# Two-layer hybrid trunk with a hierarchical mixture of experts: routing over all 32 experts at once, and a first quad fed in smaller steps

## The chip, the cores and the metric

The kernel runs on one core of one Trainium2 chip. The metric is the device time of one execution in microseconds. Several executions agree within about 0.2 per cent.

## The reference, cut to what matters

```python
D_MODEL, SEQ, DEPTH = 1024, 256, 2
N_EXPERT_GROUPS, EXPERTS_PER_GROUP, TOP_K, D_EXPERT = 4, 8, 2, 256

def hier_moe(h, w_rg, w_re, w_gate, w_up, w_down):
    t = h.reshape(b * s, d)
    pg = jax.nn.softmax((t @ w_rg).astype(jnp.float32), -1)
    pg_top, g_idx = lax.top_k(pg, 1)
    le = (t @ w_re).astype(jnp.float32).reshape(-1, N_EXPERT_GROUPS, EXPERTS_PER_GROUP)
    le_sel = jnp.take_along_axis(le, g_idx[:, :, None], axis=1)[:, 0]
    pe_top, e_idx = lax.top_k(jax.nn.softmax(le_sel, -1), TOP_K)
    w = pg_top * pe_top / jnp.sum(pe_top, -1, keepdims=True)
    ids = g_idx * EXPERTS_PER_GROUP + e_idx
    combine = jnp.sum(jax.nn.one_hot(ids, N_EXPERTS, dtype=jnp.float32) * w[..., None], 1)
    hg = jnp.einsum("nd,edf->nef", t, w_gate)
    hu = jnp.einsum("nd,edf->nef", t, w_up)
    a = jax.nn.silu(hg) * hu * combine[..., None].astype(t.dtype)
    return jnp.einsum("nef,efd->nd", a, w_down).reshape(b, s, d)

def reference(x, ...):
    for l in range(DEPTH):
        ...                                  # three gated mixer branches and w_out
        x = x + hier_moe(rms_norm(x, norm2_g[l]), w_router_group[l], w_router_expert[l],
                         w_expert_gate[l], w_expert_up[l], w_expert_down[l])
    return rms_norm(x, norm_f_g)
```

Everything is float32. One expert has three matrices of 1 MB each (1 MB is 1,048,576 bytes here), so the 32 experts of a layer are 96 MB.

## The kernel before

The program is written engine by engine with semaphores by hand; what stands in one engine's block runs in that order. Each layer is a `trunk_stage` (projection, the three mixer branches, output projection) and an `expert_stage`.

**Slots.** Expert matrices stream from DRAM into a ring of 20 places of 1 MB (`RING_E`). SyncE (SP) issues every load with `load_expert` in the order of a counter `pos`, 96 positions for a layer. A quad is four experts, and it has 12 positions: eight for gate and up matrices, four for down matrices. Positions 0 to 19 are loaded while the trunk still runs, wherever a part of the arena comes free. Position 20 goes into the place of position 0, and so on: `quads_sp` waits until TensorE has used a place, then issues the next load. For the first quad it waits for `gu_part` (positions 20 to 25) and `gu_ready` (26, 27), then for the down products `y_ready` (28 to 31); positions 32 to 39 wait for `gu_ready` of the second quad.

**The first eight positions** are cut differently (`SPLIT_LOADS`): each place holds half of the contraction blocks of two experts, gate and up, so that places 0 and 1 serve the first two of the eight contraction blocks k. Each place is filled by two loads of 512 KB, with runs of 2 KB.

**Routing** is a chain on VectorE (DVE) in `route_dve`, where `link` makes each instruction wait for the one before: group argmax, `gmask`, masked logits `big`, a sum over groups into `les`, top 2 by MAX8 and FIND_INDEX8, `pick`, `either`, `sel`. TensorE (PE) turns `sel` into ranks, and DVE builds the `onehot` matrices of the first two quads (L2079). Before `sel` is there, PE runs warm-up matmuls (`keep_clock`, L340). ScalarE (ACT) meanwhile loads two tables and computes the router's exponentials (L1670).

**The first quad** (`first_quad`): PE gathers the tokens of the four experts, one k at a time, into PSUM (`gather_pair`, L1863); ACT (L1803) or DVE (L2089) copies a pair of k to `xsel`, times the gain, and PE multiplies by the gate and up matrices (`gate_up_pair`, L1876). Pairs 0 and 2 are emptied by ACT and pairs 1 and 3 by DVE. Then follow `spread(0)` (L1913), which needs `comb_ready` from DVE's `combine_weights` (L1752 to L1766), `gather(1)` and `down(0)`.

The order of the first quad on PE before (rows of PE's program, layer 0; L1863 gathers, L1876 multiplies by gate and up, a product is one row per expert and k):

```order
L1863 MATMUL ps<-onehot,work 128x128 [waits x_copied,onehot_ready0]
L1863 MATMUL ps<-onehot,work 128x128 x7
L1876 MATMUL ps<-ring_rest,rows 32x512 [waits first_act0,expert_in0]
L1876 MATMUL ps<-ring_rest,rows 32x512 x7
L1863 MATMUL ps<-onehot,work 128x128 x4
L1876 MATMUL ps<-arena,rows 32x512 [waits first_dve0]
L1876 MATMUL ps<-arena,rows 32x512 x7
L1863 MATMUL ps<-onehot,work 128x128 x4
L1876 MATMUL ps<-arena,rows 32x512 [waits first_act0,expert_in1]
L1876 MATMUL ps<-arena,rows 32x512 x7
L1876 MATMUL ps<-arena,rows 32x512 [waits first_dve0]
L1913 MATMUL ps<-ident,onehot 128x128 [waits comb_ready]
```

All four gathers of k 0 to 3 stand ahead of the first product, and nothing stands between the products of pair 2 and those of pair 3.

Of the kernel before, what the change touches and what calls it, by code (L numbers as in the profile page):

```python
# [77 lines left out]
def trunk_program(nc, x, positions, norm1_g, w_in, b_in, attn_sinks, sgu_ln_g, sgu_ln_b, w_spatial,  # L78
# [7 lines left out]
    with ExitStack() as whole:  # L86
# [33 lines left out]
        idx_iota = sb("idx_iota", [P, PER_GROUP])  # L120
# [13 lines left out]
        with ExitStack() as ctx:  # L134
            ring_rest = sb("ring_rest", [P, (RING_E - RING_A) * SLOT], F32, ctx)
            rest_slots = ring_rest[:].rearrange("p (s n) -> p s n", n=SLOT)
            rows = sb("rows", [P, 2 * D], F32, ctx)
            h2t = rows[:].rearrange("p (k s) -> p k s", k=KB)
            xsel = rows[:, 0:D].rearrange("p (k s) -> p k s", k=KB)
            y = rows[:, D:2 * D]  # L140
            onehot = sb("onehot", [P, 2, TB, QUAD], F32, ctx)
            st_r = sb("st", [P, 2, S], F32R, ctx)
            st = st_r[:].bitcast(F32)
            acts = sb("acts", [P, 4 * F], F32, ctx)
            sg, a_sb = acts[:, 0:F], acts[:, F:2 * F]
# [6 lines left out]
            gmask = sb("gmask", [P, TB, GROUPS], F32, ctx)  # L152
            les = sb("les", [P, TB, 8], F32, ctx)
# [4 lines left out]
            pick = sb("pick", [P, TB, 2, 8], F32, ctx)  # L158
            either = sb("either", [P, TB, 8], F32, ctx)
            weighted = sb("weighted", [P, TB, 2, 8], F32, ctx)  # L160
# [18 lines left out]
        with ExitStack() as ctx:  # L179
# [10 lines left out]
            iota8_i = sb("iota8_i", [P, PER_GROUP], I32, ctx)  # L190
# [173 lines left out]
        def setup_pool(pool, link):  # L364

            pool.iota(dist_i[:, 0:P], pattern=[[-1, P]], base=0, channel_multiplier=1)
            pool.iota(dist_i[:, P:3 * P], pattern=[[-1, 2 * P]], base=P, channel_multiplier=1).then_inc(consts_ready, 1)
            link(pool.memset(ident[:], 0.0))
            pool.affine_select(out=ident[:], in_=ident[:], compare_op=ALU.not_equal, fill=1.0,
                               base=0, pattern=[[-1, P]], channel_multiplier=1).then_inc(consts_ready, 1)  # L370
            pool.iota(iota_i[:], pattern=[[1, EC]], base=1, channel_multiplier=0)
            pool.iota(iota8_i[:], pattern=[[1, PER_GROUP]], base=0, channel_multiplier=0)
# [34 lines left out]
        def rope_angles(dve, link):  # L407
# [26 lines left out]
            dve.tensor_copy(idx_iota[:], iota8_i[:])  # L434
# [16 lines left out]

        LAST_DOWN = LAYER_LOADS - 1
# [1189 lines left out]
        def expert_stage(l):  # L1642
# [62 lines left out]
            def over_groups(t):  # L1705
                return bcast(t.unsqueeze(2), [P, TB, GROUPS, PER_GROUP])

            def route_dve(dve, link):
# [16 lines left out]
                dve.max(etop[:, 0, :], les[:, 0, :])  # L1725
                link(dve.max(etop[:, 1, :], les[:, 1, :]))
                dve.max_index(top_i[:, 0, :], etop[:, 0, :], les[:, 0, :])
                link(dve.max_index(top_i[:, 1, :], etop[:, 1, :], les[:, 1, :]))
                link(dve.tensor_tensor(pick[:], bcast(idx_iota[:].unsqueeze(1).unsqueeze(1), [P, TB, 2, 8]),
                                       bcast(top_i[:, :, 0:2].unsqueeze(3), [P, TB, 2, 8]), ALU.is_equal))  # L1730
# [18 lines left out]
            def combine_weights(dve, link):  # L1749
# [8 lines left out]
                link(dve.tensor_tensor(weighted[:], pick[:], bcast(w12[:].unsqueeze(3), [P, TB, 2, 8]), ALU.mult))  # L1758
                link(dve.tensor_tensor(either[:], weighted[:, :, 0, :], weighted[:, :, 1, :], ALU.add))
                for tb in range(TB):  # L1760
                    dve.tensor_tensor(comb[:, tb, :, 0:4].rearrange("p (g h) e -> p g h e", h=2),
                                      bcast(either[:, tb, :].rearrange("p (h e) -> p h e", h=2).unsqueeze(1),
                                            [P, GROUPS, 2, 4]),
                                      bcast(gmask[:, tb, :].unsqueeze(2).unsqueeze(3), [P, GROUPS, 2, 4]),
                                      ALU.mult)
# [31 lines left out]
            def quads_act(act, R, a, b, routed):  # L1797
                def gathered(n):
                    if n == 0:
                        for i in (0, 2):  # L1800
                            act.wait_ge(R.first_ready, i + 1)
                            for k in (2 * i, 2 * i + 1):
                                last = act.activation(xsel[:, k, :], ps[:, 2 + i, (k % 2) * QUAD:(k % 2 + 1) * QUAD],  # L1803
                                                      ACT.Copy, scale=gain2[:, k:k + 1])
                            last.then_inc(R.first_act, 1)
# [9 lines left out]
                for n in range(a, b):  # L1815
# [16 lines left out]
                    if n == LAST:  # L1832
                        act.wait_ge(R.gu_part, 4)
# [24 lines left out]
            def quads_pe(pe, R, a, b, routed):  # L1858
                def gather_pair(i):

                    for k in (2 * i, 2 * i + 1):
                        for tb in range(TB):
                            mm = pe.matmul(ps[:, 2 + i, (k % 2) * QUAD:(k % 2 + 1) * QUAD],  # L1863
                                           work[:, tb, k * P:(k + 1) * P], onehot[:, 0, tb, :],
                                           start=(tb == 0), stop=(tb == 1))
                    mm.then_inc(R.first_ready, 1)

                def gate_up_pair(i):
# [3 lines left out]
                    pe.wait_ge(R.first_dve if i % 2 else R.first_act, i // 2 + 1)  # L1872
                    for k in (2 * i, 2 * i + 1):
                        for e in range(4):
                            w = first_parts(places(2 * i + e // 2)[:, 0, :])[:, e % 2, :, (k % 2) * F:(k % 2 + 1) * F]
                            mm = pe.matmul(ps[e * EC:(e + 1) * EC, 0, :].rearrange("p (a f) -> p a f", a=2),  # L1876
                                           xsel[:, k, e * EC:(e + 1) * EC], w, start=(k == 0), stop=(k == KB - 1),
                                           skip_group_check=True)
                    mm.then_inc(R.gu_part if i < 3 else R.gu_ready, 1)

                def first_quad():
# [3 lines left out]
                    gather_pair(0)  # L1885
                    gather_pair(1)
                    gate_up_pair(0)
                    gather_pair(2)
                    gate_up_pair(1)
                    gather_pair(3)  # L1890
                    gate_up_pair(2)
                    gate_up_pair(3)

                def gather(n):
                    pe.wait_ge(R.onehot_ready, n + 1)
                    if n == 1:
                        pe.wait_ge(R.first_act, 2)
                        pe.wait_ge(R.first_dve, 2)
# [173 lines left out]
            def quads_dve(dve, link, R, a, b, routed):  # L2072
# [11 lines left out]
                def gathered(n):  # L2084
                    if n == 0:
                        for i in (1, 3):
                            dve.wait_ge(R.first_ready, i + 1)
                            for k in (2 * i, 2 * i + 1):
                                last = dve.tensor_scalar(xsel[:, k, :], ps[:, 2 + i, (k % 2) * QUAD:(k % 2 + 1) * QUAD],  # L2089
                                                         gain2[:, k:k + 1], None, ALU.mult)  # L2090
                            last.then_inc(R.first_dve, 1)
# [242 lines left out]
```

## Time and profile before

| what | value |
|---|---|
| median of three runs | 1046.15 us (1045.91 to 1047.91) |
| the profiled execution | 1048.12 us, its span 1046.4 us |
| TensorE busy | 958.8 us (92%) |
| VectorE busy | 576.2 us (55%) |
| ScalarE busy | 426.7 us (41%) |
| moved by DMA | 313.04 MB, 299 GB/s on average |
| mean granted TensorE clock | 0.972 |

Times in the trace are microseconds from the span's start. Layer 0's expert stage lies at about 320 to 523 us, layer 1's at about 837 to 1040 us. "DMA share" is the busy share of the 16 DMA engines; it can read slightly over 1. The busy share of an engine is a mean over stages with different limits: the trunk keeps TensorE busy nearly all the time, the expert stages keep the DMA engines so.

### The profile page before, as it was taken

Reading aid. Unit: us, or ns where it says so; the run is one execution under the profiler, and the core shown is the slowest. Engines: PE = TensorE matmul, PEld = TensorE weight load, DVE = VectorE, ACT = ScalarE, POOL = GpSimd, SP = SyncE. Lnnn points to the kernel's source line nnn. Section 1 sums busy time; section 2 is a strip of 40 time slices with the busy share of each in tenths; the row PEclk is TensorE's granted clock in tenths of the full one; section 3 lists DMA queues with packets and bytes.
Section 4 is the critical chain, followed back from the end, with each engine's and each line's share of the span. In section 5 each row is a group of like instructions: output and inputs, shape, how many; then the busy total and the mean of one; then the engine's idle time right before and its main releaser. Section 6 shows DMA issues by size and latency. Waiting matters only on the chain.

```text
span 1046.4 us, 15393 instructions
## 1 busy us (share of the span) xinstructions
PE 958.8 (92%) x5894; PEld 668.5 (64%) x5894; DVE 576.2 (55%) x1186; ACT 426.7 (41%) x907; POOL 58.1 (6%) x74
## 2 busy tenths in 40 slices
PE   8999999999999986887899999999999999867786
PEld 6888877778886431533488887777788954333333
DVE  6765788886873321111176668898869542122212
ACT  5434566666443210111363355666664431111122
POOL 1030400000010000000003004000000100000000
PEclk9999999999999999888999999999999999989889
DMA  9965633247999999999998556332588999999996
GB/s 345 350 218 188 198 122 123 80 127 269 321 396 385 425 424 425 419 425 425 413 342 292 190 177 195 122 121 81 163 289 315 396 405 424 425 422 423 426 423 256
DMA packets 97114, 313.04 MB, mean 299 GB/s; under 512 B 13424, under 2 KB 18576, under 8 KB 74512
## 3 DMA queue, kind: packets, MB, share of 16 engines
q1 hardware_dynamic: 96704, 312.04, 78.7%
q8 instruction: 45, 0.74, 0.3%
q14 instruction: 29, 0.24, 0.1%
q10 hardware_dynamic: 336, 0.02, 0.0%
HBM read 310.20 MB, written 1.84 MB: 298 GB/s over the span
## 4 chain that ended last, share of the span: by engine, by line
PE 63%; DMA 16%; SPq 9%; DVE 6%; ACT 4%; issue 1%; DVEq 0%; ACTq 0%
PE ps L1354 14%; PE ps L1356 14%; PE ps L1355 14%; DMA arena<-in_w_expert_up_dram 10%; SPq L470 9%; DMA ring_rest<-in_w_expert_up_dram 5%; PE ps L1928 5%; PE ps L1452 2%; PE ps L1460 2%; PE ps L1903 1%; PE ps L1992 1%; PE ps L1876 1%; ACT probs L928 1%; DVE wlo L1038 1%; PE ps L1475 1%
## 5 line engine op out<-in xcount | busy, mean ns | idle before, releaser
L1354 PE MATMUL ps<-whi,ahi 128*128 128x512 f32 (+1 forms) x768 | 297.3, 387 | 6.5 <-DVE wlo L1038 5.1
L1356 PE MATMUL ps<-whi,alo 128*128 128x512 f32 (+1 forms) x768 | 289.6, 377 | 0.0
L1355 PE MATMUL ps<-wlo,ahi 128*128 128x512 f32 (+1 forms) x768 | 289.2, 377 | 0.0
L1038 DVE TENSOR_TENSOR wlo<-arena,whi 128x512 fp32r<-128x512 f32 (+1 forms) x352 | 231.5, 697 | 92.0 <-ACT whi L848 89.5
L848 ACT CAST whi<-arena 128x1024 fp32r<-128x1024 f32 (+1 forms) x176 | 180.6, 1029 | 186.5 <-PE ps L1356 186.5
L1354 PEld LDWEIGHTS ps<-whi,ahi 128*128 128x128 f32 x768 | 144.5, 188 | 38.0 <-DVE wlo L1038 7.9
L1356 PEld LDWEIGHTS ps<-whi,alo 128*128 128x128 f32 x768 | 144.4, 188 | 27.0
L1355 PEld LDWEIGHTS ps<-wlo,ahi 128*128 128x128 f32 x768 | 144.7, 188 | 24.4
L1928 PE MATMUL ps<-ring_rest,rows 128*32 128x512 f32 x320 | 95.2, 642 | 26.1 <-DMA arena<-in_w_expert_up_dram 26.1
L1928 PE MATMUL ps<-arena,rows 128*32 128x512 f32 x448 | 95.2, 662 | 10.5 <-DMA arena<-in_w_expert_up_dram 8.9
L2120 DVE SCALAR_TENSOR_TENSOR acts<-ps,wslot,acts 128x256 f32<-128x256 f32 x16 | 7.7, 484 | 162.3 <-ACT acts L1838 137.5
L1903 PE MATMUL ps<-onehot,work 128*128 128x128 f32 x448 | 58.5, 293 | 17.5 <-issue 9.1
L1838 ACT ACTIVATE acts<-ps,rslot 128x256 f32<-128x256 f32 x16 | 7.6, 475 | 161.4 <-PE ps L1928 158.5
L1903 PEld LDWEIGHTS ps<-onehot,work 128*128 128x128 f32 x448 | 55.8, 206 | 27.6 <-issue 18.3
L928 ACT ACTIVATE probs<-probs,neg 128x128 f32<-128x128 f32 x112 | 49.5, 444 | 32.7 <-DVE neg L1163 32.7
L1928 PEld LDWEIGHTS ps<-ring_rest,rows 128*32 128x32 f32 x320 | 23.2, 117 | 61.5 <-issue 61.5
L2004 PE MATMUL ps<-rows,st 128*128 128x512 f32 x112 | 54.9, 612 | 0.2
L2104 DVE TENSOR_TENSOR xs<-ps,xs 128x512 f32<-128x512 f32 x56 | 38.7, 692 | 22.7 <-PE ps L2004 22.7
L1928 PEld LDWEIGHTS ps<-arena,rows 128*32 128x32 f32 x448 | 24.3, 121 | 39.9 <-issue 39.9
L1057 DVE SCALAR_TENSOR_TENSOR arena<-ps,rstd,arena 128x512 f32<-128x512 f32 (+2 forms) x68 | 46.6, 727 | 2.2 <-PE ps L1356 2.2
L1992 PE MATMUL ps<-arena,acts 128*32 128x512 f32 x256 | 43.6, 595 | 3.7 <-ACT acts L1842 3.7
L2096 DVE TENSOR_SCALAR rows<-ps,gain 128x128 f32<-128x128 f32 x56 | 15.8, 345 | 46.8 <-PE ps L1903 46.8
(278 smaller groups left out, 1016.8 us busy)
## 6 DMA issues: line engine op xcount, KB each, us to landing
arena<-in_w_in_dram SPq DMA_DIRECT2D x62, 1024.0 KB, 5.3
arena<-in_w_expert_gate_dram SPq DMA_DIRECT2D x36, 1024.0 KB, 24.4
arena<-in_w_expert_down_dram SPq DMA_DIRECT2D x32, 1024.0 KB, 21.6
arena<-in_w_expert_up_dram SPq DMA_DIRECT2D x32, 1024.0 KB, 25.6
ring_rest<-in_w_expert_down_dram SPq DMA_DIRECT2D x28, 1024.0 KB, 13.3
ring_rest<-in_w_expert_up_dram SPq DMA_DIRECT2D x24, 1024.0 KB, 25.8
ring_rest<-in_w_expert_gate_dram SPq DMA_DIRECT2D x20, 1024.0 KB, 23.9
arena<-in_w_proj_a_dram SPq DMA_DIRECT2D x8, 1024.0 KB, 5.0
```

The source lines that it names most:

```text
L470: sp.dma_start(slot, w[l, 4 * n + e].rearrange("(p k) f -> p (k f)", p=P)).then_inc(done, 16)
L848: act.copy(whi[:, jj % 2, 0:2 * w], half_slot(jj, w)).then_inc(hi_ready, 1)
L928: act.activation(probs[:, i, n, lo:hi], probs[:, i, n, lo:hi], ACT.Exp, bias=neg[:, i, tb, n:n + 1], accum_out=den[:, i, tb, n:n + 1])
L1038: dve.tensor_tensor(wlo[:, jj % 2, cols], half_slot(jj, w)[:, cols], whi[:, jj % 2, cols].bitcast(F32), ALU.subtract).then_inc(low_split i ...
L1057: dve.scalar_tensor_tensor(out=z[:, tb, cols], in0=ps[:, bank + tb, 0:w], scalar=rstd[:, tb:tb + 1], in1=z[:, 0, cols], op0=ALU.mult, op1= ...
L1354: pe.matmul(o, hi, rhs_hi, start=first, stop=False)
L1355: pe.matmul(o, hi, rhs_lo, start=False, stop=False)
L1356: return pe.matmul(o, lo, rhs_hi, start=False, stop=last)
L1903: mm = pe.matmul(ps[:, 4 + k // 4, (k % 4) * QUAD:(k % 4 + 1) * QUAD], work[:, tb, k * P:(k + 1) * P], onehot[:, n % 2, tb, :], start=(tb ...
L1928: mm = pe.matmul(ps[e * EC:(e + 1) * EC, n % 2, :].rearrange("p (a f) -> p a f", a=2), xsel[:, k, e * EC:(e + 1) * EC], w, start=(k == 0), ...
L1992: mm = pe.matmul(ps[e * EC:(e + 1) * EC, 2 + nh, :], at_sb[:, kf, e * EC:(e + 1) * EC], w, start=(kf == 0), stop=(kf == 1), skip_group_che ...
L2004: pe.matmul(ps[:, 4 + tb, :], st[:, n % 2, tb * P:(tb + 1) * P], y[:, nh * BANK:(nh + 1) * BANK], start=True, stop=True).then_inc(R.back_r ...
```

## The change

Three parts, in both layers.

1. **Routing.** Instead of selecting the chosen group's eight logits, the logits of the other three groups are lowered by 1e30 (`others`, one scalar_tensor_tensor), and MAX8 and FIND_INDEX8 run over all 32. `les`, its TENSOR_REDUCE, `gmask` and `either` go; `pick` and `weighted` grow from 8 to 32 wide per token block and pick; `sel` is the sum of the two picks.
2. **First quad.** Each k is signalled by itself. ACT empties the even k, DVE the odd k. PE gathers k 0 to 2, multiplies pair 0, gathers 3 and 4, multiplies pair 1, gathers 5 and 6, multiplies pair 2, gathers 7, multiplies pair 3; each pair waits for both emptying engines.
3. **First two places.** Position 0 holds k = 0 and position 1 k = 1, each of all four experts (runs of 1 KB). `gu_part` is raised after k = 0 and again after k = 1, and SP waits for them one by one with positions 20 and 21.

```diff
@@ load_expert, quads_sp
+                    if pos < 2:
+                        blocks = w[l, 0:4].rearrange("e (p k) f -> p e k f", p=P)
+                        sp.dma_start(first_block(slot)[:, :, to, :], blocks[:, :, pos, :]).then_inc(done, 16)
+                        continue
...
-                        sp.wait_ge(R.gu_part, i // 2 + 1)
+                        sp.wait_ge(R.gu_part, i + 1 if i < 2 else i // 2 + 2)
@@ route_dve
-                link(dve.tensor_tensor(gmask[:], bcast(idx_iota[:, 0:GROUPS].unsqueeze(1), [P, TB, GROUPS]),
-                                       bcast(top_i[:, :, 0:1], [P, TB, GROUPS]), ALU.is_equal))
-                link(dve.tensor_tensor(
-                    by_group(big), logits[:, :, GROUPS:GROUPS + EXPERTS].rearrange("p t (g e) -> p t g e", g=GROUPS),
-                    over_experts(gmask[:]), ALU.mult))
-                link(dve.tensor_reduce(les[:], big[:].rearrange("p t (g e) -> p t e g", g=GROUPS), AX, ALU.add))
...
-                link(dve.tensor_tensor(either[:], pick[:, :, 0, :], pick[:, :, 1, :], ALU.add))
-                dve.tensor_tensor(by_group(sel), over_groups(either[:]), over_experts(gmask[:]),
-                                  ALU.mult).then_inc(picked, 1)
+                link(dve.tensor_tensor(others[:], bcast(idx_iota[:, 0:GROUPS].unsqueeze(1), [P, TB, GROUPS]),
+                                       bcast(top_i[:, :, 0:1], [P, TB, GROUPS]), ALU.not_equal))
+                link(dve.scalar_tensor_tensor(
+                    out=by_group(big), in0=over_experts(others[:]), scalar=NEG,
+                    in1=logits[:, :, GROUPS:GROUPS + EXPERTS].rearrange("p t (g e) -> p t g e", g=GROUPS),
+                    op0=ALU.mult, op1=ALU.add))
...
+                dve.tensor_tensor(sel[:], pick[:, :, 0, :], pick[:, :, 1, :], ALU.add).then_inc(picked, 1)
@@ quads_act, quads_dve, gathered(0)
+                        for k in range(0, KB, 2):
+                            act.wait_ge(R.first_ready, k + 1)
+                            act.activation(xsel[:, k, :], first_place(k), ACT.Copy,
+                                           scale=gain2[:, k:k + 1]).then_inc(R.first_act, 1)
...
+                        for k in range(1, KB, 2):
+                            dve.wait_ge(R.first_ready, k + 1)
+                            dve.tensor_scalar(xsel[:, k, :], first_place(k), gain2[:, k:k + 1], None,
+                                              ALU.mult).then_inc(R.first_dve, 1)
@@ gate_up_pair
-                    pe.wait_ge(R.first_dve if i % 2 else R.first_act, i // 2 + 1)
+                    pe.wait_ge(R.first_act, i + 1)
+                    pe.wait_ge(R.first_dve, i + 1)
...
+                        if k == 0:
+                            mm.then_inc(R.gu_part, 1)
```

PE's program at the same place, changed kernel (L1862 gathers, L1878 multiplies by gate and up):

```order
L1862 MATMUL ps<-onehot,work 128x128 [waits x_copied,onehot_ready0]
L1862 MATMUL ps<-onehot,work 128x128 x5
L1878 MATMUL ps<-ring_rest,rows 32x512 [waits first_dve0,first_act0,expert_in0]
L1878 MATMUL ps<-ring_rest,rows 32x512 x7
L1862 MATMUL ps<-onehot,work 128x128 x4
L1878 MATMUL ps<-arena,rows 32x512 [waits first_dve0,first_act0]
L1878 MATMUL ps<-arena,rows 32x512 x7
L1862 MATMUL ps<-onehot,work 128x128 x4
L1878 MATMUL ps<-arena,rows 32x512 [waits first_dve0,first_act0,expert_in1]
L1878 MATMUL ps<-arena,rows 32x512 x7
L1862 MATMUL ps<-onehot,work 128x128 x2
L1878 MATMUL ps<-arena,rows 32x512 [waits first_dve0,first_act0]
```

One k's gather (two rows) has moved from ahead of the first product to a place between the products of pairs 2 and 3, and every pair now waits for both engines.

## Rows read from the trace of the kernel before

**Rows 1.** Windows: engines' busy us, PE clock, DMA share, GB/s; long stretches.

```profile
282.00:328.00 46.00, 45.34 (x293) 38.69 (x291) 31.00 (x73) 20.21 (x34) 4.92 (x4) 1.00 1.01 383
332.00:513.00 181.00, 146.80 (x1081) 70.09 (x1080) 41.09 (x105) 30.80 (x109) 0.00 (x0) 0.93 1.01 423
```

**Rows 2.** Windows: the two short stretches in which the stream thins out, and one within.

```profile
328.00:330.50 2.50, 2.50 (x26) 1.32 (x24) 0.00 (x0) 0.63 (x2) 0.00 (x0) 1.00 0.80 243
...
328.00:328.50 0.50, 0.50 (x7) 0.50 (x6) 0.00 (x0) 0.00 (x0) 0.00 (x0) 1.00 0.94 393
...
844.50:847.00 2.50, 2.50 (x27) 1.39 (x24) 0.00 (x0) 0.63 (x2) 0.00 (x0) 1.00 0.73 229
```

**Rows 3.** Chain that ended last: start us, us, what; around layer 1's last matrices.

```profile
1000.50 26.80 DMA ring_rest<-in_w_expert_up_dram
```

**Rows 4.** Timeline of SP's queue: start us, us, line, load; after routing.

```profile
328.07 0.80 SPq L470 DMA_DIRECT2D ring_rest<-in_w_expert_down_dram  x2
...
344.40 0.33 SPq L470 DMA_DIRECT2D arena<-in_w_expert_gate_dram  x1
...
355.91 1.75 SPq L470 DMA_DIRECT2D ring_rest<-in_w_expert_down_dram  x4
...
844.71 0.80 SPq L470 DMA_DIRECT2D ring_rest<-in_w_expert_down_dram  x2
```

**Rows 5.** Timeline of all engines, routing of layer 0.

```profile
319.52 3.27 PE L340 MATMUL ps<-wr,ident 128*128 128x256 f32 x14
...
321.07 0.26 DVE L1724 TENSOR_REDUCE les<-big 128x16 f32<-128x64 f32 x1
...
321.36 0.17 DVE L1725 MAX8 etop<-les 128x8 f32<-128x8 f32 x1
...
322.27 0.17 DVE L1731 TENSOR_TENSOR either<-pick 128x16 f32<-128x16 f32 x1
322.47 0.22 DVE L1732 TENSOR_TENSOR sel<-either,gmask 128x64 fp32r<-128x64 f32 x1
...
325.30 0.63 ACT L1803 ACTIVATE rows<-ps,gain 128x128 f32<-128x128 f32 x2
```

**Rows 6.** Timeline of PE, the first quad of layer 0.

```profile
324.10 2.05 PE L1863 MATMUL ps<-onehot,work 128*128 128x128 f32 x16
326.08 1.92 PE L1876 MATMUL ps<-ring_rest,rows 128*32 128x512 f32 x16
327.94 1.16 PE L1863 MATMUL ps<-onehot,work 128*128 128x128 f32 x8
329.03 1.92 PE L1876 MATMUL ps<-arena,rows 128*32 128x512 f32 x16
...
331.97 3.64 PE L1876 MATMUL ps<-arena,rows 128*32 128x512 f32 x32
335.54 0.44 PE L1913 MATMUL ps<-ident,onehot 128*128 128x128 f32 x2
```

**Rows 7.** Timeline of DVE: the weights of the first quad, first instruction and last.

```profile
332.60 0.15 DVE L1752 TENSOR_REDUCE pg<-lse 128x2 f32<-128x8 f32 x1
...
334.22 0.18 DVE L1766 COPY comb<-rstd 128x16 f32<-128x16 f32 x1
```

**Rows 8.** By line: duration in ns, min/median/max; first and last start.

```profile
L1803 ACT ACTIVATE rows<-ps,gain x8: 360/364/369, 325.3 to 846.0; 128x128 f32<-128x128 f32 x8
...
L2089 DVE TENSOR_SCALAR rows<-ps,gain x8: 340/348/353, 326.2 to 849.0; 128x128 f32<-128x128 f32 x8
```

**Rows 9.** Windows: a load in 1 KB runs (L711), 2 KB runs, two lulls.

```profile
192.00:193.00 1.00, 1.00 (x6) 0.81 (x5) 0.93 (x4) 0.04 (x1) 0.00 (x0) 1.00 1.05 372
256.00:270.00 14.00, 14.00 (x64) 11.58 (x63) 9.98 (x16) 9.28 (x11) 0.00 (x0) 1.00 1.05 393
278.00:282.00 4.00, 4.00 (x20) 3.30 (x19) 3.73 (x7) 2.10 (x2) 0.00 (x0) 1.00 0.42 156
796.00:800.00 4.00, 4.00 (x20) 3.30 (x19) 3.87 (x7) 1.05 (x1) 0.00 (x0) 1.00 0.28 73
```

More of the change, by code:

```diff
@@ L157, in trunk_program @@
             w12 = sb("w12", [P, TB, 2], F32, ctx)
-            pick = sb("pick", [P, TB, 2, 8], F32, ctx)
-            either = sb("either", [P, TB, 8], F32, ctx)
-            weighted = sb("weighted", [P, TB, 2, 8], F32, ctx)
+            picks = acts[:, 3 * F:].rearrange("p (n t i e) -> p n t i e", n=2, t=TB, i=2)
+            pick, weighted = picks[:, 0], picks[:, 1]
             sel = sb("sel", [P, TB, EXPERTS], F32R, ctx)
@@ L450, in first_parts, with first_block, first_place @@
             return slot.rearrange("p (e a n) -> p e a n", e=2, a=2)
+        def first_block(slot):
+            return slot.rearrange("p (e a f) -> p e a f", e=4, a=2)
+        def first_place(k):
+            return ps[:, 2 + k % 4, (k // 4) * QUAD:(k // 4 + 1) * QUAD]
         LAST_DOWN = LAYER_LOADS - 1
@@ new lines, in route_dve @@
+                dve.max(etop[:, 0, :], big[:, 0, :])
+                link(dve.max(etop[:, 1, :], big[:, 1, :]))
+                dve.max_index(top_i[:, 0, :], etop[:, 0, :], big[:, 0, :])
+                link(dve.max_index(top_i[:, 1, :], etop[:, 1, :], big[:, 1, :]))
+                link(dve.tensor_tensor(pick, bcast(idx_iota[:].unsqueeze(1).unsqueeze(1), [P, TB, 2, EXPERTS]),
+                                       bcast(top_i[:, :, 0:2].unsqueeze(3), [P, TB, 2, EXPERTS]), ALU.is_equal))
+                dve.tensor_tensor(sel[:], pick[:, :, 0, :], pick[:, :, 1, :], ALU.add).then_inc(picked, 1)
@@ L1757, in combine_weights @@
                 link(dve.tensor_tensor(w12[:, :, 1], w12[:, :, 0], lse[:, :, GROUPS + 1], ALU.mult))
-                link(dve.tensor_tensor(weighted[:], pick[:], bcast(w12[:].unsqueeze(3), [P, TB, 2, 8]), ALU.mult))
-                link(dve.tensor_tensor(either[:], weighted[:, :, 0, :], weighted[:, :, 1, :], ALU.add))
+                link(dve.tensor_tensor(weighted, pick, bcast(w12[:].unsqueeze(3), [P, TB, 2, EXPERTS]), ALU.mult))
                 for tb in range(TB):
[L1761 to L1765, printed above, removed]
+                    dve.tensor_tensor(comb[:, tb, :, 0:4], weighted[:, tb, 0, :].rearrange("p (n e) -> p n e", e=4),
+                                      weighted[:, tb, 1, :].rearrange("p (n e) -> p n e", e=4), ALU.add)
                 dve.tensor_copy(comb[:, :, :, 4], bcast(rstd[:].unsqueeze(2), [P, TB, QUADS])).then_inc(comb_ready, 1)
@@ L1799, in gathered @@
                     if n == 0:
[L1800 to L1805, printed above, removed]
+                        for k in range(0, KB, 2):
+                            act.wait_ge(R.first_ready, k + 1)
+                            act.activation(xsel[:, k, :], first_place(k), ACT.Copy,
+                                           scale=gain2[:, k:k + 1]).then_inc(R.first_act, 1)
                         return
@@ L1858, in quads_pe, with gather_first @@
             def quads_pe(pe, R, a, b, routed):
-                def gather_pair(i):
-                    for k in (2 * i, 2 * i + 1):
+                def gather_first(*ks):
+                    for k in ks:
                         for tb in range(TB):
-                            mm = pe.matmul(ps[:, 2 + i, (k % 2) * QUAD:(k % 2 + 1) * QUAD],
-                                           work[:, tb, k * P:(k + 1) * P], onehot[:, 0, tb, :],
+                            mm = pe.matmul(first_place(k), work[:, tb, k * P:(k + 1) * P], onehot[:, 0, tb, :],
                                            start=(tb == 0), stop=(tb == 1))
-                    mm.then_inc(R.first_ready, 1)
+                        mm.then_inc(R.first_ready, 1)
                 def gate_up_pair(i):
@@ L1871, in gate_up_pair @@
                         wait_weights(pe, 2 * i, routed)
-                    pe.wait_ge(R.first_dve if i % 2 else R.first_act, i // 2 + 1)
+                    pe.wait_ge(R.first_act, i + 1)
+                    pe.wait_ge(R.first_dve, i + 1)
                     for k in (2 * i, 2 * i + 1):
                         for e in range(4):
-                            w = first_parts(places(2 * i + e // 2)[:, 0, :])[:, e % 2, :, (k % 2) * F:(k % 2 + 1) * F]
+                            if i == 0:
+                                w = first_block(places(k)[:, 0, :])[:, e, :, :]
+                            else:
+                                w = first_parts(places(2 * i + e // 2)[:, 0, :])[:, e % 2, :, (k % 2) * F:(k % 2 + 1) * F]
                             mm = pe.matmul(ps[e * EC:(e + 1) * EC, 0, :].rearrange("p (a f) -> p a f", a=2),
@@ L1884, in first_quad @@
                         pe.wait_ge(x_copied, 1)
[L1885 to L1886 removed]
+                    gather_first(0, 1, 2)
                     gate_up_pair(0)
[L1888 removed]
+                    gather_first(3, 4)
                     gate_up_pair(1)
[L1890 removed]
+                    gather_first(5, 6)
                     gate_up_pair(2)
+                    gather_first(7)
                     gate_up_pair(3)
```

31 lines of the change are left out of this document (8 added, 23 removed).

## The prediction, made before the changed kernel was run

> **What bounds the kernel now.** I read the windows first. Through the expert stage the DMA engines are busy all the time and move 423 GB/s, while TensorE is busy 147 of 181 us; before routing they are busy too, at 383 GB/s [rows 1]. The chain of waits says the same at its end: layer 1's last up matrix takes 26.8 us from issue to landing, which is a long queue and not a slow load, and PE waits for it [rows 3]. So from 282 us on, layer 0 ends when its bytes have passed, and faster routing, gathering or multiplying is worth nothing in itself. Only time in which the stream is idle can be won.
>
> There is one such hole per layer. Around 328 us the first 20 places are full and the stream runs dry: from 328.0 to 330.5 it moves 243 GB/s instead of 423, so 2.5 x (1 - 243/423) = 1.06 us of streaming are lost; in layer 1 it is 2.5 x (1 - 229/423) = 1.15 us [rows 2]. The next load waits for the first pair of k to be used and is issued at 328.07 [rows 4]. The first half us of that window still moves 393 GB/s [rows 2], so the stream runs until about 328.5. The window holds 608 KB in all, 1.44 us of streaming, of which 0.46 us is in that half us; the other 0.97 us before 330.5 means that the new loads count as full stream from 329.53, **1.46 us after their issue**. Layer 1's issue stands 516.64 us later at 844.71 [rows 4], so its stream resumes at 846.17, and the bytes of its window put its drying at 845.02.
>
> The upper bound of what the change can give is therefore 1.06 + 1.15 = **2.21 us**.
>
> **Routing.** The TENSOR_REDUCE takes 321.07 to the next start at 321.36, 0.29 us, and `either` takes 322.27 to 322.47, 0.20 us [rows 5]: 0.49 us removed. Added: a DVE instruction with 16 elements per partition takes 0.17 us and one with 64 takes 0.22 us [rows 5], about 1 ns an element. Two MAX8 and two FIND_INDEX8 over 24 more elements are 0.10 us, `pick` with 96 more 0.10 us, the scalar_tensor_tensor in place of a product some 0.03 us. Net: `sel` 0.26 us earlier. PE can't use all of that. Its 14 warm-up records start at 319.52 and end at 322.79 [rows 5], so the first rank product can follow at about 322.6, only some 0.13 us earlier than now. But ACT's table, root and exponential hang on DVE alone, so ACT is free at 325.04 instead of 325.30 [rows 5]. The wider `weighted` (+0.10 us) stands against the removed `either` (0.2 us) in the weights' chain.
>
> **First quad, start.** The first product waits now for two copies on ACT (0.63 us [rows 5]) and starts at 326.08 [rows 6], 0.15 us after them. After the change one copy of 0.364 us [rows 8] does, from 325.04, and PE starts at 325.55, **0.53 us earlier**. DVE's k = 1 is no later: PE gathers from 324.10 [rows 6] less 0.13, at 0.12 us a matmul record it has two k after about 1.1 us, and the DVE copy of 0.348 us [rows 8] ends at 325.48.
>
> **First quad, first load.** A pair's products occupy PE 1.86 us (326.08 to 327.94 [rows 6]), one k half of that. The place of k = 0 is free at 325.55 + 0.93, and with the 0.13 us that lie between the next PE start and the issue now, SP issues at **326.61 instead of 328.07**. With 1.46 us until the bytes count, 328.07 is before 328.5: the hole is closed, with 0.43 us to spare. Layer 1: 843.25 + 1.46 = 844.71 against 845.02. Position 21 follows 0.93 us later and 1 MB lasts 2.48 us at 423 GB/s, so nothing is late there.
>
> **First quad, end.** Here the change costs. Gathering two k between pairs takes 1.09 us (327.94 to 329.03 [rows 6]) as before, and the copy of the odd k (0.348 us) just fits beside the second one's gather. But k = 7 is now gathered between pairs 2 and 3, and pair 3 waits for its copy: 0.64 us for the gather to end, 0.35 us for the copy, 0.1 us of semaphores, 1.09 us in all, where nothing stood. Going through: pair 0 from 325.55, pair 1 at 328.50, pair 2 at 331.45, k = 7's gather at 333.31, pair 3 at 334.40 and its end at 336.23, against 335.54 now [rows 6]: PE's path comes out **0.69 us later**. The weights' chain on DVE takes from 332.60 to 334.40 [rows 7], 1.8 us, and would start at 334.3 after k = 7's copy; it ends at about 336.1, just under the same cover.
>
> **Does that lateness cost anything?** Only if the stream runs dry again. Positions 20 to 27 are issued by 336.5, 28 to 31 at 344.40, 32 onward at 355.91 [rows 4]. After the change the stream runs from 328.5: 8 MB reach to 348.3, and the issue at 345.09 + 1.46 = 346.55 is in time. 12 MB reach to 328.5 + 29.75 = 358.25, and the issue at 356.60 + 1.46 = 358.06 is in time by 0.19 us; in layer 1, 845.02 + 29.75 = 874.77 against 874.70, in time by 0.07 us. So this is the **second hole in waiting**: every 0.1 us by which PE is later than I reckon, beyond that, is given back, once in each layer. Later points are far from it, since 20 MB are issued by then and PE waits for data.
>
> **The 1 KB runs.** Two MB per layer are loaded in runs of half the length. The trace has a load in such runs, which reaches 372 GB/s, and 2 KB runs in a full stream 393 [rows 9]: 5.6 us instead of 5.3 us, +0.3 us. They are loaded near 250 and 767 us, and the stream has lulls behind them: from 278 to 282 its share is 0.42, from 796 to 800 it is 0.28 [rows 9], so 2.3 and 2.9 us are idle. PE never waits for trunk weights there. Cost: nothing, up to an excess of 2.3 us.
>
> **Sum.** Against the profiled execution of 1048.12 us: at most -2.21 us. Four handovers (two per layer) have margins of 0.43, 0.31, 0.19 and 0.07 us, and the 16 DMA engines don't run dry at one moment; I charge 0.13 us for each, an estimate by choice, and come to **-1.7 us**. Bounds: 0, if the second hole opens by as much as the first closes, and -2.2. The profiled execution lies 2.0 us above the median of the runs; the change is the same against either, so 1046.15 - 1.7 = 1044.4.
>
> A rule stands against one number here. The rows give 1.46 us from issue to effective stream. The Trainium skill (DMA: Bandwidth & Descriptors, Latency and other measured facts) gives about 600 ns to the first byte for this kind of queue. The trace's number is much larger, and by the page's figure all four margins would be 0.86 us wider, no handover would cost anything and the estimate would be -2.2 us.
>
> **The rivals.** *Full closure* (-2.2 us, 1043.9): the handovers cost nothing, because loads that meet running engines start sooner than those that meet idle ones. For it: the tail of the dry stream is still 393 of 423. Against: margins of tenths. By that rule of the page it would come out so. *Second hole* (-0.5 us, 1045.6): PE's path is late by 1.3 us or more instead of 0.69, by the semaphores of a pair that now waits for two engines, or because the weights' chain outlasts pair 3. Then 0.6 to 0.9 us per layer come back at 358 and 875. It decides from 0.88 us of lateness on in layer 0 and from 0.76 in layer 1. For it: two new waits on PE and no spare time. Also here: routing no faster, because PE's warm-up or the wide searches hold it; the first hole then still closes, but PE is 0.26 us later. *Short runs clog the stream* (slower, +2.7 us, 1048.9): the two places loaded in 1 KB pieces move at 200 GB/s, since each piece lies 8 KB from the next. 2.1 MB then take 10.5 us, 5.2 more; 2.3 and 2.9 us of that fall into the lulls, 2.9 and 2.3 push everything up to the first hole, which gives 1.1 each: +1.8 and +1.2, less the tenths of the handovers. It decides from 2.3 + 1.06 = 3.4 us of excess, a rate of some 240 GB/s. Against it: 372 GB/s on the load in such runs.
>
> **How the numbers follow.** Forecast (-1.3 to -2.1 us) 0.45, full closure 0.22, second hole 0.24, short runs 0.09. The likeliest gives 1044.4. The range runs from full closure less some scatter of the runs, 1043.6, to the second hole at no gain with the same scatter, 1046.4. A measurement of this kernel tells 0.2 per cent, 2.1 us, from no change. Full closure and a part of the forecast lie beyond it: faster 0.30; slower 0.08; the same 0.62.
>
> **What would show it.** In the changed profile: no stretch under 400 GB/s from 327 to 331 and 843 to 848; the first load after routing issued 1.3 to 1.6 us earlier; pair 3 preceded by a wait of PE of about 0.45 us for DVE; `spread(0)` 0.5 to 0.9 us later; the stream full at 356 to 360. Wrong if the place of k = 0 is freed late, if the stream thins again near 358 or 875, or if PE waits for data in the trunk.

## The result and the profile after

The changed kernel is slower: 1049.48 us median (1047.42 to 1051.77, ten runs) against 1047.03 us (1045.91 to 1047.96, ten runs), a ratio of 1.0021 with a 95% interval of 1.0013 to 1.0029. The forecast was 1044.4 us in a range up to 1046.4. In a second comparison, the first experiment below, it was 1.0018 (1.0007 to 1.0029).

First the stream. These are windows of the changed kernel in the columns of [rows 1] (busy us and counts of PE, weight loads, DVE, ACT, POOL; PE clock; DMA share; GB/s): the stretch before routing, and the two long ones of the expert stages. The line by itself is layer 1's stretch in the kernel before.

```profile
282.00:328.00 46.00, 45.24 (x291) 38.83 (x289) 30.93 (x71) 20.60 (x35) 4.91 (x4) 1.00 0.99 380
...
332.00:513.00 181.00, 147.03 (x1082) 70.43 (x1082) 40.90 (x104) 31.16 (x110) 0.00 (x0) 0.92 1.01 420
...
849.00:1030.00 181.00, 148.76 (x1064) 69.62 (x1063) 41.09 (x104) 31.16 (x110) 0.00 (x0) 0.92 1.01 420
```
```profile
849.00:1030.00 181.00, 149.69 (x1108) 70.92 (x1104) 40.81 (x105) 30.79 (x109) 0.00 (x0) 0.92 1.01 424
```

The DMA engines are as busy as before (share 1.01) and move 420 GB/s where they moved 423 [rows 1] and 424. That is 0.7 to 0.9 per cent over two times some 180 us, or **1.3 to 1.7 us in each layer**, more than the whole loss. It has no place of its own: it lies over both stages.

Then the place where the gain was to come from. SP's issues after routing, changed kernel:

```profile
327.21 1.19 SPq L480 DMA_DIRECT2D ring_rest<-in_w_expert_down_dram  x2
331.17 1.08 SPq L480 DMA_DIRECT2D arena<-in_w_expert_down_dram  x2
...
357.63 1.75 SPq L480 DMA_DIRECT2D ring_rest<-in_w_expert_down_dram  x4
```

And the stream around it, in windows of half a microsecond, and last one of four microseconds around the second quad's loads:

```profile
328.00:328.50 0.50, 0.50 (x7) 0.50 (x5) 0.00 (x0) 0.00 (x0) 0.00 (x0) 1.00 1.00 426
...
329.00:329.50 0.50, 0.41 (x5) 0.19 (x8) 0.05 (x1) 0.35 (x1) 0.00 (x0) 1.00 0.95 246
329.50:330.00 0.50, 0.50 (x8) 0.15 (x4) 0.00 (x0) 0.02 (x1) 0.00 (x0) 1.00 0.79 147
330.00:330.50 0.50, 0.50 (x9) 0.16 (x4) 0.00 (x0) 0.00 (x0) 0.00 (x0) 1.00 0.74 229
330.50:331.00 0.50, 0.50 (x8) 0.00 (x0) 0.00 (x0) 0.00 (x0) 0.00 (x0) 1.00 0.72 279
331.00:331.50 0.50, 0.50 (x8) 0.45 (x5) 0.00 (x0) 0.00 (x0) 0.00 (x0) 1.00 0.83 295
...
357.00:361.00 4.00, 4.00 (x39) 3.50 (x32) 0.48 (x1) 1.62 (x5) 0.00 (x0) 1.00 1.02 426
```

The logits' copy, and with it all of this stage, lies 0.53 us later than in the profile of the kernel before (320.25 against 319.73, rounded). Less that, the first load is issued at 326.68, where 326.61 was forecast, against 328.07 [rows 4]. And yet the stream thins out for more than two microseconds. Measured over the 8 us that start 6 us after the router's logits are copied, the hole costs 1.28 us in layer 0 and 1.18 us in layer 1 before, and 1.42 and 1.16 us in this profile (8 us times one less the window's rate over that of the 30 us behind it). The windows for layer 0, before and then after, are:

```profile
325.70:333.70 8.00, 8.00 (x69) 3.58 (x71) 2.06 (x10) 0.85 (x3) 0.00 (x0) 1.00 0.93 356
333.70:363.70 30.00, 29.06 (x236) 14.52 (x228) 9.03 (x34) 8.17 (x27) 0.00 (x0) 1.00 1.01 424
```
```profile
326.30:334.30 8.00, 7.82 (x65) 3.39 (x58) 0.70 (x2) 0.85 (x3) 0.00 (x0) 1.00 0.94 348
334.30:364.30 30.00, 28.52 (x228) 14.84 (x232) 10.15 (x39) 7.86 (x27) 0.00 (x0) 1.00 1.01 423
```

Last, the engines: the changed kernel's routing and first quad (answers to [rows 5, 6]).

```profile
320.05 3.27 PE L338 MATMUL ps<-wr,ident 128*128 128x256 f32 x14
...
321.59 0.20 DVE L1732 MAX8 etop<-big 128x8 f32<-128x32 f32 x1
...
322.37 0.29 DVE L1736 TENSOR_TENSOR acts<-idx_iota,top_i 128x128 f32<-128x128 f32 x1
322.70 0.23 DVE L1738 TENSOR_TENSOR sel<-acts 128x64 fp32r<-128x64 f32 x1
...
325.40 0.35 ACT L1803 ACTIVATE rows<-ps,gain 128x128 f32<-128x128 f32 x1
325.60 0.35 DVE L2092 TENSOR_SCALAR rows<-ps,gain 128x128 f32<-128x128 f32 x1 [0.85 <-PE ps L1862]
...
326.10 1.92 PE L1878 MATMUL ps<-ring_rest,rows 128*32 128x512 f32 x16
...
329.20 1.93 PE L1878 MATMUL ps<-arena,rows 128*32 128x512 f32 x16
...
332.30 1.92 PE L1878 MATMUL ps<-arena,rows 128*32 128x512 f32 x16
...
335.40 1.92 PE L1878 MATMUL ps<-arena,rows 128*32 128x512 f32 x16 [0.54 <-DVE rows L2092]
...
337.26 0.44 PE L1917 MATMUL ps<-ident,onehot 128*128 128x128 f32 x2
```

`sel` starts 2.45 us after the logits' copy and started 2.74 us after it before: 0.29 us earlier, forecast 0.26. PE's first product is at 325.57 on the old time scale (forecast 325.55). The end of the first quad is at 336.73 on that scale, 1.19 us later than the 335.54 of [rows 6], not 0.69.

### The profile page after: what moved, and what is told of

Same layout as the page of the kernel before. It is cut to its first block, busy times and chain, and to the rows that moved or that the text cites. A ratio compares the mean times of both kernels' runs of the same rounds, so it can differ in the third digit from the quotient of the medians.

```text
span 1050.1 us, 15391 instructions
## 1 busy us (share of the span) xinstructions
PE 961.2 (92%) x5894; PEld 669.4 (64%) x5894; DVE 575.4 (55%) x1180; ACT 426.7 (41%) x907; POOL 58.2 (6%) x74
## 4 chain that ended last, share of the span: by engine, by line
PE 62%; DMA 16%; SPq 10%; DVE 6%; ACT 3%; issue 2%; DVEq 0%; ACTq 0%
PE ps L1364 14%; PE ps L1366 14%; PE ps L1365 14%; DMA arena<-in_w_expert_up_dram 10%; SPq L480 9%; PE ps L1932 5%; DMA ring_rest<-in_w_expert_up_dram 3%; DMA ring_rest<-in_w_expert_down_dram 3%; PE ps L1462 2%; PE ps L1470 2%; DVE wlo L1048 1%; PE ps L1878 1%; PE ps L1907 1%; PE ps L1996 1%; ACT probs L938 1%
```

## The experiments

Theories after the result. **A**: one single load into a dry stream leaves the DMA engines out of step. **B**: the memory rate scatters by itself. **C**: PE's later first quad costs. The first four kernels take the change apart.

### The change and its three parts, each alone

The parts are those of the diff above, each put alone into the kernel before: routing (`only_route`), the gathers in smaller steps with two emptying engines (`only_quad`), and the first two places with SP's single waits (`only_slots`):

```diff
# only_slots, beside first_block and load_expert as in the change
-                        sp.wait_ge(R.gu_part, i // 2 + 1)
+                        sp.wait_ge(R.gu_part, i + 1 if i < 2 else i // 2 + 2)
...
+                            if i == 0:
+                                w = first_block(places(k)[:, 0, :])[:, e, :, :]
```

> The whole change once more, beside its parts. Theory A, the stream's start: the profile of the changed kernel shows a hole that is flatter but not smaller, and afterwards a stream at 420 instead of 424 GB/s. If one single load that starts a dry stream leaves the 16 DMA engines out of step, 418 to 421 GB/s come again here: +1 to +4 us against before. Theory B, scatter of the memory rate that has nothing to do with the change: 423 to 424 GB/s in this profile, within 1 us of before. Theory C, PE's path: it is 1.19 us later at the end of the first quad, not 0.69, and this lateness is what costs; again +1 to +3 us.

> Routing over all 32 experts alone; first quad and places as before. Sel 0.26 us earlier moves the whole first quad by up to 0.3 us towards the dry point of the stream. Theories A and C: the hole shrinks by 0.3 us a layer, -0.2 to -0.6 us. Theory B: within 0.7 us of before.

> First quad gathered in smaller steps and emptied by both engines; routing, places and SP's waits as before. PE starts 0.25 us earlier and is about 1.4 us later at the end of the first quad. Theory C: slower by 1 us or more, with a thin stretch near 358 or 875 us. Theory A: the first load is issued about 0.2 us earlier in the old pattern of two at once, so -0.5 to +0.5 us. Theory B: the same.

> Places 0 and 1 hold one k of four experts each, loaded in 1 KB runs, and SP issues positions 20 and 21 one by one; routing and first quad's gathers as before. Theory A: all of the loss is here, +1 to +4 us, stream at 418 to 421 GB/s after the hole. Theories B and C: the first load is 0.9 us earlier, so up to -0.9 us a layer, -1.8 us in all.

| kernel | ratio to before | 95% interval |
|---|---|---|
| whole change, again | 1.0018 | 1.0007 to 1.0029 |
| routing alone | 1.0020 | 1.0011 to 1.0028 |
| first quad alone | 1.0003 | 0.9994 to 1.0011 |
| first two places alone | 0.9991 | 0.9981 to 1.0001 |

All of the loss is in the part that should matter least. A and C fall: the kernels that hold the single load or the long first quad don't lose. B falls with them: the whole change again moved 420 GB/s in both stages, and so did routing alone, while the other two parts stayed at the rate of the kernel before. The windows of the kernel before, of routing alone, and of the places alone:

```profile
340.00:513.00 173.00, 138.80 (x1010) 64.72 (x1009) 37.60 (x82) 27.28 (x98) 0.00 (x0) 0.93 1.01 424
857.00:1030.00 173.00, 141.81 (x1036) 65.63 (x1040) 37.36 (x82) 27.00 (x97) 0.00 (x0) 0.91 1.01 424
```

```profile
340.00:513.00 173.00, 141.42 (x1040) 66.41 (x1036) 36.03 (x76) 26.66 (x96) 0.00 (x0) 0.91 1.01 420
857.00:1030.00 173.00, 142.34 (x1030) 64.53 (x1022) 36.15 (x77) 26.20 (x96) 0.00 (x0) 0.91 1.01 420
```
```profile
340.00:513.00 173.00, 140.06 (x1036) 67.88 (x1038) 37.57 (x82) 27.40 (x99) 0.00 (x0) 0.92 1.01 424
857.00:1030.00 173.00, 142.93 (x1042) 66.03 (x1034) 36.52 (x77) 26.92 (x97) 0.00 (x0) 0.92 1.01 423
```

Routing runs for a few microseconds; it can't slow a stream for the 180 us behind it. But the new routing needs an index row of 32 elements where there were 8, and `idx_iota` is allocated ahead of `ring_rest`. The 96 more bytes per partition move everything behind it. **Theory D**: what costs is the address of the places, the buffers' pieces of 1 MB (8192 bytes in each partition) into which the loads write. The start addresses in a partition, from the allocator:

| kernel | arena (12 places) | over 256 | ring_rest (8 places) | over 256 |
|---|---|---|---|---|
| before, first quad alone, places alone | 32928 | 160 | 145152 | 0 |
| changed, routing alone | 32928 | 160 | 145248 | 96 |

"Over 256" is what the start is past a multiple of 256. Since 8192 is such a multiple, all places of a buffer stand alike to this grid.

### The address alone, and repaired

```diff
# shift_only: the kernel before, and nothing else
         idx_iota = sb("idx_iota", [P, PER_GROUP])
+        sb("shift", [P, 24])
# route_64: routing alone; changed_256: the whole change
         idx_iota = sb("idx_iota", [P, EXPERTS])
+        sb("shift", [P, 8])        # route_64
+        sb("shift", [P, 40])       # changed_256
# arena_64: the kernel before; warm takes 32 bytes in a partition
-        warm = sb("warm", [P, 1])
         arena = sb("arena", [P, TB * D_IN + RING_T * SLOT])
+        warm = sb("warm", [P, 1])
```

> The kernel before with nothing changed but 96 unused bytes per partition behind idx_iota, which is what the wider index row of the changed kernel does to every tensor allocated after it: the places in ring_rest start at byte 145248 (32 past a multiple of 64) instead of 145152 (a multiple of 256). Theory D, placement: the stream falls from 424 to 420 GB/s and the time rises by 1.5 to 2.5 us, as with the new routing alone. If instead the routing's instructions cost it: within 0.7 us of before and 424 GB/s.

> The new routing alone, with 32 more unused bytes, so that ring_rest starts at 145280: a multiple of 64, but 128 past a multiple of 256. Theory D with a grid of 64 bytes: 424 GB/s and -0.2 to -0.6 us against before (what routing was to bring). Theory D with a grid of 256 bytes: 420 to 422 GB/s and +1 to +2 us. If placement has nothing to do with it: +1.9 us as with the new routing alone.

> The whole change, with 160 more unused bytes, so that ring_rest starts at 145408, a multiple of 256 again. Theory D: 424 GB/s, and the change is worth what its parts without the shift give: 0 to -1 us against before, 1.9 us less than the whole change. If placement has nothing to do with it: +1.8 us.

> The kernel before with the 4-byte tensor warm allocated behind the arena instead of ahead of it: the arena, with 12 of the 20 places, starts at 32896, a multiple of 64 (128 past one of 256), instead of 32928; everything behind it stays. Theory D with a grid of 64: 12 of 20 places gain what 8 of 20 lost, so 424 becomes some 430 GB/s and the time falls by 2.5 to 4 us. With a grid of 256: no change or up to -1 us. If placement has nothing to do with it: within 0.7 us.

| kernel | arena over 256 | ring_rest over 256 | ratio to before | 95% interval | GB/s in the two stages |
|---|---|---|---|---|---|
| shift_only | 160 | 96 | 1.0025 | 1.0015 to 1.0035 | 420, 421 |
| route_64 | 160 | 128 | 1.0016 | 1.0007 to 1.0026 | 420, 421 |
| changed_256 | 160 | 0 | 0.9997 | 0.9988 to 1.0006 | 423, 423 |
| arena_64 | 128 | 0 | 1.0000 | 0.9992 to 1.0009 | 424, 424 |

The rows of shift_only, in which not one instruction differs from the kernel before:

```profile
340.00:513.00 173.00, 140.65 (x1022) 65.87 (x1025) 37.68 (x83) 27.68 (x100) 0.00 (x0) 0.91 1.01 420
857.00:1030.00 173.00, 139.27 (x1008) 63.33 (x1004) 36.55 (x79) 26.67 (x96) 0.00 (x0) 0.92 1.01 421
```

and of the whole change with ring_rest back on a multiple of 256:

```profile
340.00:513.00 173.00, 142.72 (x1050) 70.17 (x1053) 38.05 (x83) 29.70 (x103) 0.00 (x0) 0.92 1.01 423
857.00:1030.00 173.00, 142.03 (x1050) 63.93 (x1050) 37.37 (x82) 26.59 (x97) 0.00 (x0) 0.93 1.01 423
```

That the addresses cost it is shown from both sides: 96 unused bytes cost what the change cost, and 160 more give it back. Of the two grids in question it is the one of 256: 128 bytes off it costs about as much as 96 bytes off, though it is a multiple of 64, and moving the arena from one off-grid place to another changes nothing.

That it is the places which pay is argued. The same bytes also move everything behind `ring_rest`, and TensorE, ScalarE and VectorE use some of that in the expert stages: `rows` (with `xsel` and `y`), `onehot`, `st`, `acts`. No run moved these without `ring_rest`. For the places speaks that the rate of the stream falls, while TensorE has time to spare (141 of 173 us busy).

The Trainium skill (DMA: Bandwidth & Descriptors, How a descriptor splits into AXI transactions) says that a piece which doesn't start on a multiple of 256 bytes begins with a transaction at the multiple below, and that the bytes fetched ahead of its start are unused and still cost beats on the bus; it says so of reading. The runs show the same grid where the side that is written was moved.

### The arena too

If 8 places off the grid cost this much, the 12 of the arena have always cost something.

```diff
# before_both_256; changed_both_256 and slots_both_256 likewise (the second padding 16 in the changed kernel)
+        sb("shift_ahead", [P, 24])
         arena = sb("arena", [P, TB * D_IN + RING_T * SLOT])
...
         idx_iota = sb("idx_iota", [P, PER_GROUP])
+        sb("shift", [P, 40])
# route_256: routing alone, the row of 32
+        sb("shift", [P, 40])
```

> The new routing alone, ring_rest at 145408, a multiple of 256. Placement theory: 424 GB/s; the shorter DVE chain moves the first load some 0.2 us nearer to the dry point, so -0.2 to -0.5 us against before, and 1.5 to 2.5 us less than the new routing without the padding. Rival, the routing's own instructions or their timing cost it: +1 us or more.

> The kernel before with 96 unused bytes ahead of the arena and 160 behind idx_iota: the arena (12 of 20 places) starts at 33024 and ring_rest at 145408, both multiples of 256; before, the arena is 160 past one. If every place off the grid costs as the 8 places of ring_rest did (424 to 420 GB/s, +1.9 to +2.6 us), the stream rises to some 430 GB/s and the time falls by 2.5 to 4 us. If the loss needs an address that is also off a smaller grid, or ring_rest only: within 0.7 us of before.

> The whole change with both buffers at multiples of 256. If the arena's placement counts: the gain of both kernels before it together, -3 to -5 us, and the best so far. If not: as the whole change with ring_rest alone aligned, 0 to -1 us.

> Only the new first two places, with SP's single waits, and both buffers at multiples of 256. The places alone gave -0.9 us; with the arena's part -3.5 to -5 us. Against the whole change so placed it tells what the longer first quad (PE 1.2 us later) costs: 0.3 to 0.8 us less than that one.

These came out at 0.9996 (0.9987 to 1.0005), 0.9984 (0.9975 to 0.9993), 0.9974 (0.9964 to 0.9984) and 0.9972 (0.9960 to 0.9984). Routing on the grid costs nothing that these runs can tell. The kernel before, with nothing but addresses moved, is 0.16 per cent faster: 1.7 us, less than the expected 2.5 to 4. The other two also fell short of what was expected (3 to 5 and 3.5 to 5 us): they gained 2.7 and 2.9 us. The windows of before_both_256:

```profile
340.00:513.00 173.00, 143.18 (x1073) 67.47 (x1073) 37.20 (x81) 26.82 (x97) 0.00 (x0) 0.92 1.01 426
857.00:1030.00 173.00, 142.87 (x1045) 66.12 (x1047) 36.24 (x77) 27.71 (x97) 0.00 (x0) 0.90 1.01 424
```

The stream gains 0.5 per cent at most with 12 places moved onto the grid, where it lost 0.9 per cent with 8 moved off it. So the cost isn't proportional to the number of places; why, is open. The bytes put ahead of the arena also move the small tiles between the two buffers, `ident` among them, so here too the places are argued.

### What the parts are worth on the grid

The gain that was forecast had still not shown by itself, so four kernels with both buffers on the grid were set beside each other on one chip: the kernel before, the whole change, the places alone, and routing with places but the old first quad.

> The new first two places alone, both buffers at multiples of 256, once more beside the three others on one chip. If the first load's 0.9 us count: 0.8 to 1.4 us less than the kernel before so placed (-2.6 to -3.2 us against before). If the whole gain is placement: equal to it.

> The kernel before with both buffers at multiples of 256, once more: -1 to -2.5 us against before, a stream of 424 to 426 GB/s.

> The whole change so placed, once more. If the second hole at the second quad (seen as 1 to 2 us at 330 to 390 GB/s) gives back what the first load gains: between the kernel before so placed and the places alone, 0.3 to 1 us above the latter. If it costs nothing: equal to the places alone or up to 0.5 us below.

> Routing and first two places, but the first quad's gathers as before, both buffers at multiples of 256: the first load is about as early as in the whole change (0.9 + 0.2 us), and PE ends the first quad early, so no second hole. If the holes are all that counts: the fastest of the four, 0 to 0.5 us below the places alone. If routing itself costs: above them.

| on the grid | first comparison | second comparison |
|---|---|---|
| before | 0.9984 (0.9975 to 0.9993) | 0.9984 (0.9974 to 0.9994) |
| whole change | 0.9974 (0.9964 to 0.9984) | 0.9979 (0.9968 to 0.9990) |
| places alone | 0.9972 (0.9960 to 0.9984) | 0.9974 (0.9965 to 0.9984) |
| routing and places | | 0.9976 (0.9967 to 0.9985) |

The places alone are below their base three times: by 0.9 (off the grid), 1.2 and 1.0 thousandths, some 1 us. Each difference is within its intervals; it is their agreement that speaks. What routing adds, and what the longer first quad takes, is smaller than these runs can tell: routing and places, which was to be the fastest if only the holes counted, is level with the places alone.

The profiles show where it goes. For each kernel and layer, the loss in the first hole as defined above:

| kernels | us lost in the first hole (both layers of each profile) | mean |
|---|---|---|
| old places: nine profiles | 1.28 1.18, 2.58 1.21, 1.27 1.74, 1.08 1.08, 1.00 1.70, 1.30 0.68, 1.03 2.28, 0.78 2.12, 0.90 2.30 | 1.42 |
| new places: nine profiles | 1.42 1.16, 0.27 0.65, 0.31 0.52, 0.72 1.49, 0.95 1.25, 0.65 0.56, 0.62 0.68, 0.75 0.79, 1.05 0.75 | 0.81 |

So the earlier first load takes 0.6 us from the hole in each layer and doesn't close it: 1.2 us in all, which agrees with the 1 us measured. In the profile of the changed kernel itself (the first of the lower row) it happened to be as deep as before.

Part of the scatter has a place. In four of the 36 stages PE's first rank product follows `sel` by 1.4 us or more (under 0.3 us in the profile of the kernel before), and the first load comes later by as much. One is arena_64, layer 0, with a hole of 2.58 us: its copy of the logits is at 320.49, so its first load comes 9.80 us after it, where the kernel before takes 8.34.

```profile
330.29 0.80 SPq L470 DMA_DIRECT2D ring_rest<-in_w_expert_down_dram  x2
```

The others are only_quad (2.12), before_both_b (2.30) and changed_both_256 (1.49), all in layer 1. What holds PE there wasn't looked into. Without the four the means are 1.23 and 0.77 us: 0.5 us a layer, 0.9 us in all.

And the second hole opened. The four microseconds around the second quad's loads in changed_256, layer 1, and single microseconds in the whole change's second profile, layer 0:

```profile
873.00:877.00 4.00, 3.54 (x33) 3.19 (x36) 1.18 (x5) 1.52 (x5) 0.00 (x0) 1.00 0.95 377
```
```profile
358.00:359.00 1.00, 1.00 (x12) 1.00 (x11) 0.20 (x1) 0.00 (x0) 0.00 (x0) 1.00 1.01 369
359.00:360.00 1.00, 1.00 (x12) 1.00 (x11) 0.00 (x0) 0.78 (x4) 0.00 (x0) 1.00 0.94 352
```

Over 6 us from 36 us after the logits' copy, the five profiles of the whole change move 393 to 422 GB/s, 410 on average; eight profiles without the new first quad move 418 to 436, 424 on average. That is 6 x (1 - 410/424) = 0.2 us a layer (the first quad alone, in neither group, moves 411 and 423 GB/s). Two of the five are off the grid, which by itself takes some 4 GB/s from them; the three others move 409 on average. It is a rival's mechanism at a third of its price or less.

## Why the prediction was wrong, point by point

- **What bounds the kernel**: right. The DMA stream sets both expert stages in every profile, and only what touched the stream moved the time.
- **The term that failed is one that the sum doesn't have.** The diff widens a small tile that stands ahead of `ring_rest`, and the prediction counted that tile's instructions and not its 96 bytes. What they move costs 2.1 to 2.6 us (routing alone 1.0020, shift_only 1.0025), about as much as the 2.21 us that were the upper bound of the gain. Less the 0.3 to 1.0 us that the change is worth without it, this leaves a loss of 1.1 to 2.3 us; measured were 1.9 and 2.2 (1.0018 and 1.0021). "Cost: nothing" was reckoned for the stream's packets by their length alone [rows 9]; where they are written wasn't asked. None of the rivals had it; the one on the slower side, 1 KB runs, had another mechanism.
- **The 1 KB runs**: right that they cost nothing. From 256 to 270 us the stream was slower (371 GB/s against the 393 of [rows 9]), and the lull behind, 278 to 282 us, took it up: its share rose from 0.42 to 0.61. The places alone are not slower (0.9991).

```profile
256.00:270.00 14.00, 14.00 (x67) 11.68 (x66) 9.85 (x16) 9.75 (x10) 0.00 (x0) 1.00 1.03 371
...
278.00:282.00 4.00, 4.00 (x20) 3.30 (x18) 3.83 (x7) 1.71 (x2) 0.00 (x0) 1.00 0.61 232
```

- **Routing**: right, 0.29 us against 0.26. Worth nothing in time, as said.
- **First load**: its issue was right within 0.1 us. Wrong was the step "1.46 us until the bytes count as full stream", and with it that a load issued so much ahead of the dry point closes the hole. That number came from two loads issued together; here one comes, and the second 0.9 us behind it. In this profile the stream then runs at 147 to 295 GB/s from 329.0 to 331.5, over 4 us after the issue. In changed_256 (layer 0, issue at 327.94) it thins for one microsecond only, to 311 and 328 GB/s, and is back at 393 by 330.5, still 2.5 us after the issue. So the change brings 0.9 to 1.2 us instead of 2.2. The test that was named, no stretch under 400 GB/s from 327 to 331, failed at once. So did the rival of full closure: each of the 18 stages with the new places loses between 0.27 and 1.49 us. Whether it is the single load that makes the difference is argued; no run issued two loads so early.

```profile
329.50:330.00 0.50, 0.41 (x8) 0.25 (x10) 0.28 (x1) 0.12 (x1) 0.00 (x0) 1.00 0.90 311
330.00:330.50 0.50, 0.50 (x8) 0.23 (x12) 0.00 (x0) 0.24 (x1) 0.00 (x0) 1.00 0.92 328
330.50:331.00 0.50, 0.50 (x12) 0.17 (x6) 0.00 (x0) 0.00 (x0) 0.00 (x0) 1.00 0.94 393
```

- **First quad's end**: 1.19 us late instead of 0.69. The copy of the odd k starts 0.75 us after its gather's first matmul, and PE waits for it 0.1 to 0.2 us before each pair, not just the last; over three pairs this is the half microsecond. The price, the second hole, was named. By the prediction's thresholds of 0.88 and 0.76 us, a lateness of 1.19 gives back 0.3 us in layer 0 and 0.4 in layer 1; 0.2 us a layer were measured. The 0.6 to 0.9 us that the rival put at a lateness of 1.3 don't follow from these thresholds, which give 0.4 and 0.5.
- **The handovers**: the charge of 0.5 us for four of them was far too small for the first and about right for the second. Without the placement the change is 0.3 to 1.0 thousandths faster (changed_256 0.9997; on the grid 0.9974 and 0.9979 against 0.9984), not 1.6, and none of the three differences is clear of its intervals.

## What to carry to other kernels

A change that resizes any tile can move every tile behind it. Where a DMA stream sets the time, compare the start addresses of its buffers before and after, and keep them on multiples of 256 bytes; two lines of unused bytes gave this kernel 1.7 us by themselves, and 2.7 to 2.9 us together with the new first two places (0.9972 and 0.9974 of before), more than anything that moved an instruction. When an edit loses in a stage that it doesn't touch, test it with its bytes alone and its instructions away.

## What the runs showed of the hardware

- A stream of loads in pieces of 8 KB, 8 of its 20 places starting 96 or 128 bytes past a multiple of 256 and the other 12 off the grid too: 420 to 421 GB/s. The 8 at a multiple: 423 to 424. All 20 at one: 424 to 426, in windows that the stream fills. The share of busy DMA engines is 1.01 in each case, so the busy share doesn't show it and only the rate does.
- Tiles that lie over `ring_rest` in the trunk share its addresses, but aren't in use in the expert stages, where the rate falls. The engines' tiles behind it are, and moved by the same bytes; a kernel that moves one and not the other wasn't run.
- A load of 1 MB that is issued 1.5 us ahead of the point where the stream thins out doesn't keep it full: 147 to 295 GB/s for two and a half microseconds in one profile, 311 and 328 GB/s for one in another, in windows of half a microsecond. How the 16 engines share one load wasn't looked into.
- The hole's depth scatters between profiles of kernels with the same instructions (before, arena_64, shift_only, and before_both_256 and before_both_b), from 0.9 to 2.6 us. A single profile is no measure of it.
